# A two-layer encoder trunk on one core: where the differences of weight blocks in the down projection are made and kept

## What is computed

```python
h2 = rms_norm(x, g_ffn_pre[i])
u = causal_dwconv(h2 @ w_up[i], conv_w[i], conv_b[i])
ug, uv = u[..., :D_FF], u[..., D_FF:]
f = (jax.nn.gelu(ug, approximate=True) * uv) @ w_down[i]     # 512 x 2816 times 2816 x 1024
x = x + rms_norm(f, g_ffn_post[i])
```

## Time and profile before

| | |
|---|---|
| median of three runs | 1831.44 us |
| profiled execution, whole | 1827.23 us |
| its span, first to last instruction | 1825.4 us |
| TensorE matmul busy | 1809.3 us (99%) |
| VectorE busy | 1190.9 us (65%) |
| ScalarE busy | 935.3 us (51%) |
| GpSimd busy | 346.0 us (19%) |
| DMA moved | 253.43 MB, mean 139 GB/s |
| mean granted TensorE clock | 0.996 of 2.4 GHz |

### The profile page before, as it was taken

How to read it: one execution, slowest core, us unless ns; L and a number is a source line. 1 busy time by engine, 2 the same in 40 slices (tenths; PEclk the granted TensorE clock), 3 DMA queues, 4 the chain that set the end, 5 groups by cost and what they waited for, 6 DMA issues and landing times.

```text
span 1825.4 us, 26834 instructions
## 1 busy us (share of the span) xinstructions
PE 1809.3 (99%) x9111; PEld 1506.8 (83%) x9111; DVE 1190.9 (65%) x1800; ACT 935.3 (51%) x1660; POOL 346.0 (19%) x314
## 2 busy tenths in 40 slices
PE   9999999999999999999999999999999999999998
PEld 8888888788888888887898888887888888888877
DVE  4756555555577777886656565555455887778874
ACT  4676546533454444555547764466334444445563
POOL 1002001132023334301010020012221244332010
PEclk9999999999999999999999999999999999999999
DMA  6322354479424333685253224545893333337842
GB/s 185 77 82 82 100 115 121 117 192 281 133 80 119 109 118 112 215 286 187 91 150 88 65 82 113 106 130 123 208 275 92 101 109 117 113 116 252 276 143 92
DMA packets 312392, 253.43 MB, mean 139 GB/s; under 512 B 65092, under 2 KB 265440, under 8 KB 312032
## 3 DMA queue, kind: packets, MB, share of 16 engines
q1 hardware_dynamic: 301160, 222.51, 40.6%
q0 software_dynamic: 10752, 29.36, 7.2%
q10 hardware_dynamic: 376, 0.21, 0.1%
HBM read 236.76 MB, written 42.47 MB: 153 GB/s over the span
## 4 chain that ended last, share of the span: by engine, by line
PE 95%; DMA 2%; DVE 2%; issue 0%; ACT 0%; DVEq 0%; POOL 0%; POOLq 0%; ACTq 0%; SPq 0%
PE psum L888 85%; PE psum L1203 2%; DMA raw<-in_w_down_dram 2%; PE psum L1184 2%; PE psum L1169 2%; PE psum L931 1%; PE psum L1156 1%; PE psum L1155 1%; DVE dn_wl L1981 0%; PE psum L1181 0%; PE psum L1166 0%; PE psum L1395 0%; DVE raw L2066 0%; PE psum L1165 0%; DVE dn_ll L1981 0%
## 5 line engine op out<-in xcount | busy, mean ns | idle before, releaser
L888 PE MATMUL psum<-xnh,wh 128*128 128x512 f32 (+1 forms) x1424 | 564.1, 396 | 0.0
L888 PE MATMUL psum<-xnh,wl 128*128 128x512 f32 (+1 forms) x1424 | 548.9, 385 | 0.0
L888 PE MATMUL psum<-xnl,wh 128*128 128x512 f32 (+1 forms) x1424 | 548.3, 385 | 0.0
L1514 ACT ACTIVATE wh<-raw 128x1024 fp32r<-128x1024 f32 (+2 forms) x276 | 284.6, 1033 | 495.3 <-PE psum L888 454.6
L1981 DVE TENSOR_TENSOR wl<-raw,wh 128x1024 fp32r<-128x1024 f32 (+2 forms) x276 | 364.5, 1322 | 150.1 <-ACT wh L1514 149.9
L888 PEld LDWEIGHTS psum<-xnh,wl 128*128 128x128 f32 x1424 | 267.6, 188 | 54.3
L888 PEld LDWEIGHTS psum<-xnh,wh 128*128 128x128 f32 x1424 | 269.1, 189 | 50.1 <-issue 2.7
L888 PEld LDWEIGHTS psum<-xnl,wh 128*128 128x128 f32 x1424 | 268.3, 188 | 46.9
L2219 DVE CUSTOM_DVE_ANT_0 Sp<-psum,ptok 128x128 f32<-128x128 f32 (+3 forms) x128 | 62.8, 491 | 108.4 <-issue 60.3
L2734 POOL TENSOR_TENSOR merged<-merged,th 128x512 f32<-128x512 f32 x32 | 46.8, 1463 | 265.8 <-DVE th L2351 265.7
L2431 DVE TENSOR_TENSOR ub<-psum,rb 128x512 f32<-128x512 f32 x88 | 60.6, 688 | 39.9 <-PE psum L888 39.9
(11 more groups left out here) (333 smaller groups left out, 3477.8 us busy)
## 6 DMA issues: line engine op xcount, KB each, us to landing
raw<-in_w_up_dram SPq DMA_DIRECT2D x88, 512.0 KB, 3.8
raw<-in_w_gate_dram SPq DMA_DIRECT2D x48, 512.0 KB, 3.8
col_sums<-in_w_down_dram POOLq DMA_DIRECT2D x44, 512.0 KB, 8.4
raw<-in_w_down_dram SPq DMA_DIRECT2D x44, 512.0 KB, 4.8
raw<-in_w_in_dram SPq DMA_DIRECT2D x30, 512.0 KB, 3.7
raw<-col_sums SPq DMA_DIRECT2D x22, 512.0 KB, 4.4
qspill<-f_sums SPq DMA_DIRECT2D x22, 384.0 KB, 4.8
q_raw<-qspill SPq DMA_DIRECT2D x22, 384.0 KB, 5.4
```

The costliest lines, as they stand in the source:

```text
L888: ins = pe.matmul(out, left, right, start=start and n == 0, stop=stop and n == 2)
L1514: act.activation(halves(c)[0][:, 0:n], raw[s][:, 0:n], ACT.Copy).then_inc(w_hi.sem, 1)
```

## The change

The difference of the diagonal blocks is made in the first round for pairs 2 to 10 (`DIFF_FROM = 2`), when `dn_raw` is on chip anyway: `lo` calls the new `diff_away`, ahead of its wait for `hi`. The result (128 x 512) goes to one of two buffers `diff_out` at 28 and 30 KB of `in_xn`, which lie over the last part of `ydn`. SyncE stores it to a DRAM tensor `diffs` behind the load four chunks later. In the second round the `dn_diff` chunk of these pairs is loaded from `diffs`, 256 KB instead of 512, and ScalarE takes it as it lands. For pairs 0 and 1 all stays as it was. `threes_taken` waits until all stores have landed, since it writes `ydn`.

```diff
@@
+DIFF_FROM = 2
@@
-    diff_made = Tally(sem("diff_made"), PAIRS)
+    diff_made = Tally(sem("diff_made"), DIFF_FROM)
+    diff_apart = Tally(sem("diff_apart"), PAIRS - DIFF_FROM)
+    diff_kept = [Tally(sem(f"diff_kept{i}"), 16 * len(range(DIFF_FROM + i, PAIRS, 2))) for i in range(2)]
@@
+    diff_out = [in_xn(f"diff_out{i}", 28 + 2 * i, [P, 512]) for i in range(2)]
@@
+    diffs = nc.dram_tensor("diffs", [DEPTH, P, PAIRS, D // 2], F32, kind="Internal").ap()
@@ def chunk_dmas(L, c):
+        if kind == "dn_diff" and m >= DIFF_FROM:
+            return [(r[:, 0:512], diffs[L, :, m, :])]
         if kind in ("dn_raw", "dn_diff"):
@@ def load(L, c):
             wait(w_lo.sem, w_lo.at(L, c - RAW + 1))
+            if CHUNKS[c][0] == "dn_diff" and CHUNKS[c][1] >= DIFF_FROM:
+                k = CHUNKS[c][1] - DIFF_FROM
+                wait(diff_kept[k % 2].sem, diff_kept[k % 2].at(L, 16 * (k // 2 + 1)))
@@ SyncE, behind the loads of q_raw
+                for k in range(PAIRS - DIFF_FROM):
+                    if c == ST_DOWN + 2 * (k + DIFF_FROM) + 4:
+                        wait(diff_apart.sem, diff_apart.at(L, k + 1))
+                        sp.dma_start(diffs[L, :, k + DIFF_FROM, :], diff_out[k % 2][:, :]).then_inc(diff_kept[k % 2].sem, 16)
@@ ScalarE, hi(L, c)
-            if CHUNKS[c][0] == "dn_diff":
+            if CHUNKS[c][0] == "dn_diff" and CHUNKS[c][1] < DIFF_FROM:
                 act.wait_ge(diff_made.sem, diff_made.at(L, CHUNKS[c][1] + 1))
@@ VectorE, lo(L, c)
             if CHUNKS[c][0] == "dn_raw" and CHUNKS[c][1] >= ROWS:
                 rows_sum(L, c)
+            if CHUNKS[c][0] == "dn_raw" and CHUNKS[c][1] >= DIFF_FROM:
+                diff_away(L, c)
             dve.wait_ge(w_hi.sem, w_hi.at(L, c + 1) + it * 4)
@@
+        def diff_away(L, c):
+
+            k, s = CHUNKS[c][1] - DIFF_FROM, (L * NCH + c) % RAW
+            dve.wait_ge(w_landed[s], LAND[L * NCH + c])
+            if k == 0:
+                dve.wait_ge(w_used.sem, w_used.at(L, ST_DOWN))
+            if k >= 2:
+                dve.wait_ge(diff_kept[k % 2].sem, diff_kept[k % 2].at(L, 16 * (k // 2)))
+            dve.tensor_tensor(diff_out[k % 2][:, :], raw[s][:, 0:512], raw[s][:, 512:1024], ALU.subtract
+                              ).then_inc(diff_apart.sem, 1)
@@ def threes_taken(L, a):
             if a == 0:
                 dve.wait_ge(q_lo.sem, q_lo.at(L, PAIRS))
+                for k in range(2):
+                    dve.wait_ge(diff_kept[k].sem, diff_kept[k].at(L, diff_kept[k].per))
@@ def down_chunks(L):
-                if q >= 0 and q % 2 == 0:
+                if q >= 0 and q % 2 == 0 and q // 2 < DIFF_FROM:
                     diff(L, q // 2)
```

## The result

The changed kernel is slower. In one session twelve runs of it gave a median of 1832.67 us (1831.31 to 1834.60) and twelve runs of the kernel before 1829.24 us; the ratio is 1.0020, 95% interval 1.0011 to 1.0029, or +3.4 us. The forecast was 1825.1 us, a gain of 6.3 on the median of 1831.44 shown ahead of it. The profiled execution of the changed kernel took 1833.82 us, its span is 1832.0, and the granted clock is 0.999 in the mean (before 0.996).

What follows compares the result with a forecast made beforehand. TensorE was taken as the bound, with gain possible only at its stalls in the two down-projection tails. A 12.3 us gain less 6.0 us of first-round cost gave -6.3 us, from 1831.4 to 1825.1 us, range 1820.0 to 1834.0.

Steps and rivals of the forecast that it cites:

- the larger of the two and not the sum: First round: delay is the larger of VectorE's and DMA's costs, 4.8 us in the first layer, 4.0 in the second.
- covers of 1.8 and 1.0 us: Turn of the rounds: lo(24) is ready 1.8 and 1.0 us before TensorE wants chunk 24, leaving 3.0 us stall per layer.
- VectorE's own 4.8 us: First round: eight added subtractions at 0.60 us; bounds 4.0 to 4.8 us in the first layer, 2.8 to 4.8 in the second.
- The DMA part: First round: nine 256 KB stores take 6.8 us per layer; free share absorbs some, leaving 4.8 and 3.2 us of delay.
- The ceiling: Both layers' tails: stalls of 3.66 and 4.73 us plus slow-clock losses of 2.7 and 2.4, 13.5 us together.
- The tail: End of the second round: 0.6 us of stall left per layer, slow clock gone; gain 12.3 us.
- The first subtraction: First round: the first of nine falls into VectorE's 1.44 us wait for ScalarE before 753.75 and costs nothing.
- At chunk 6: First round: first TensorE stall, 0.8 us if VectorE and GpSimd take turns, none by shared bandwidth; no change to the total.
- A: Rival, first round: DMA engines have no room, stores cost 6.8 us in each layer; 1829.9 us, chance 0.20.
- C: Rival, turn of rounds: last store lands late, threes_taken waits, one 6.6 us stall lowers the clock; 1837.3 us, chance 0.09.
- D: Rival, tail: not relieved since load 42 goes out no earlier, 0.8 us gained per layer; 1835.8 us, chance 0.09.
- B: Rival, first round: VectorE's idle time hides cost, stalls 4.0 us, tail's 0.6 vanish; 1821.9 us, chance 0.14.

Runs made afterwards that it cites:

- e1: Changed kernel with subtractions whole but each store cut to 8 columns, second round loading 256 KB chunks from w_down: 1826.36 us, ratio 0.9980 to before.
- e2: Changed kernel with the nine stores per layer whole but each subtraction cut to 8 columns: 1829.17 us, ratio 1.0000 to before.
- e3: Changed kernel without subtractions, stores and their waits, second round loading 256 KB chunks from w_down: 1820.30 us, ratio 0.9943 to before.
- e10: Changed kernel without subtractions and stores, second round loading half blocks of w_down, ScalarE's embedding output ahead of its last x_sum: 1817.15 us, ratio 0.9934 to before.
- e8: Changed kernel with seven of eleven 384 KB loads of spilled feature sums per layer cut to 8 columns: 1826.82 us, ratio 0.9987 to before.
- e6: Kernel before, with VectorE in the tail making the column chunk's low half ahead of the next chunk's difference: 1828.78 us, ratio 1.0000.
- e4: Changed kernel with DIFF_FROM = 8, so only the last three pairs' differences are made in the first round: 1829.53 us, ratio 0.9995 to before.
- e9: Changed kernel with DIFF_FROM = 5 (six differences per layer) and ScalarE's embedding output ahead of its last x_sum: 1827.02 us, ratio 0.9989 to before.
- e11: Changed kernel with DIFF_FROM = 6 (five differences per layer) and ScalarE's embedding output ahead of its last x_sum: 1825.11 us, ratio 0.9979 to before.
- e12: Changed kernel with DIFF_FROM = 7 (four differences per layer) and ScalarE's embedding output ahead of its last x_sum: 1824.68 us, ratio 0.9977 to before.

## Why the prediction was wrong

**The step that failed.** It is this one: "DMA and VectorE are filled by the same pace and not one after the other, so I take the larger of the two and not the sum: 4.8 us of delay in the first layer, 4.0 in the second". Measured from the down projection's first matmul, `lo(24)` started after 60.9 us in before and after 69.7 us in the changed kernel:

```profile
801.41 1.23 DVE L2075 TENSOR_TENSOR raw<-raw 128x1024 f32<-128x1024 f32 x1 [1.60 <-DMA raw<-in_w_down_dram]
...
811.62 0.69 DVE L2093 TENSOR_TENSOR raw<-raw 128x512 f32<-128x512 f32 x1 [2.04 <-DMA raw<-in_w_down_dram]
...
814.62 1.81 DVE L1997 TENSOR_TENSOR wl<-raw,wh 128x1024 fp32r<-128x1024 f32 x2
```

That is a delay of 8.8 us, and 7.7 in the second layer. The last row is `lo(24)` itself; the two above show VectorE idle for loads that have not landed, 2.04 us of it ahead of `diff(1)`. With the forecast's covers of 1.8 and 1.0 us the stalls should be 7.0 and 6.7 us; the table has 6.9 and 6.6. The same rule fits e1 (delays 4.3 and 4.1 us, so 2.5 and 3.1; table 2.5 and 3.1) and e2 (5.7 and 5.2, so 3.9 and 4.2; table 3.9 and 4.3). The covers were right, the delay was not. In the second layer the forecast didn't even keep to its own rule: 4.0 lies between VectorE's highest value and DMA's 3.2 and is the larger of no two terms.

**Why the costs add.** Taken against e3, whose second round is the same, the delays of `lo(24)` are 3.2 and 2.5 us by VectorE alone, 4.6 and 3.6 by the stores alone, and 7.6 and 6.1 by both: sums to within 0.2 us. So close a match is partly luck, for e3 itself has `lo(24)` 1.2 and 1.5 us later than before, though it makes the same first round, and e10, with that first round again, 0.5 later and 0.4 earlier; single executions scatter by 1 to 1.5 us. Against before the two alone add up to 10.0 and 9.3, and both together are 8.8 and 7.7. By either reckoning both are 2.5 to 3.1 us above the larger of the two, which is more than the scatter.

Why would they add? What follows is my reading of it. The maximum would hold for two resources that each have their own stock of work. Here there are four `raw` buffers and one circle: `lo` frees a buffer, SyncE issues the load, the load lands, VectorE adds, subtracts and splits, and `lo` frees the buffer. A longer landing and longer work on VectorE are passed one after the other by the same buffer. That the share of the DMA engines stays at 0.95 and VectorE's busy time falls to 37.83 of 40 us fits this. The runs show that the costs add, and e8 that taking other bytes away brings the period back to that of the subtractions alone; that the circle of four buffers is the reason is not shown. A run with a fifth buffer would test it directly; none was made.

**Its terms.** VectorE's own 4.8 us in the first layer was right in size (4.3 in e1; second layer 4.1 in a range of 2.8 to 4.8). The DMA part was forecast at 4.8 and 3.2; e2 has 5.7 and 5.2 against before, 4.6 and 3.6 against e3, so at most a part of it was missing. The rate was not what failed (337 GB/s at a share of 0.99). How much of the free share of 2.0 and 3.6 us took up stores these figures can't tell. The rise in landing time shows the cost of the stores from the side of DMA. Issues of the changed kernel in 757 to 800 (count, KB each, us to landing); the 256 KB loads took 4.8 and the 512 KB ones 5.1 in the same stretch of before:

```profile
raw<-in_w_down_dram SPq DMA_DIRECT2D x14, 256.0 KB, 5.5
raw<-in_w_down_dram SPq DMA_DIRECT2D x6, 512.0 KB, 5.7
diffs<-diff_out SPq DMA_DIRECT2D x7, 256.0 KB, 5.9
```

**A term that was missing.** The embedding's stall, 2.8 us in both layers, stood in no step. In before TensorE came to the embedding 18.6 us behind the start of the tail, held up by the stall and the slow clock; without them it comes 13.5 us behind it, and `ple_out` behind its `x_sum` is late. The forecast let the gain end at the tail and didn't ask what is late next behind it. Against the table the parts add up: the stalls of the first round and the turn are 7.5 us more than forecast, the embedding costs 2.8, and the tail's gain is 1.3 less; that is 11.6 in all, between the forecast's -6.3 and the table's 18.5 - 13.3 = +5.2.

**What was right.** The ceiling: 13.5 us forecast, 13.3 in the table. The tail: 0.6 us of stall left per layer was forecast, 1.2 and 1.1 are, and the clock is at 1.00, the 2.4 GHz level, in both. So the gain is 11.0 us in the tail against a forecast of 12.3, and 8.2 with the embedding's 2.8 taken off (e3, which pays nothing in the first round: 7.8 in the table, 9.6 in the medians). The first subtraction fell into VectorE's idle time: it starts at 752.70, and the idle time ahead of the next split falls from 1.44 to 0.83 us. At chunk 6 the forecast set 0.8 us by turns with GpSimd and none by a shared bandwidth. VectorE in time:

```profile
756.49 1.76 DVE L2075 TENSOR_TENSOR raw<-raw 128x1024 f32<-128x1024 f32 x1
758.17 1.78 DVE L2086 TENSOR_TENSOR diff_out<-raw 128x512 f32<-128x512 f32 x1
759.87 3.98 DVE L1997 TENSOR_TENSOR dn_wl<-raw,dn_wh 128x1024 fp32r<-128x1024 f32 x2
```

The subtraction took 1.78 us, where its median over 18 is 0.69, beside GpSimd operations of 1.7 to 2.3 us, and the first stall of the round is at 762.29, 0.99 us over the pace (1.01 in the second layer). In e2 the subtraction of 8 columns took 1.25 us in this place, and 0.16 in most others. Both operations were 1.09 us longer beside GpSimd, so the wait doesn't shrink with the operation; and e2 has no stall at chunk 6. The Trainium skill (SBUF — State Buffer, Who interferes with whom) has a VectorE `tensor_tensor` with both inputs in SBUF and a GpSimd operation that reads SBUF exclude each other, and the trace agrees in place and size.

Of its signs, the DMA share of the second round fell (0.68 in 806 to 846, before 0.81) and that of the first stayed at 0.95. The sums of rows were to come every 5.5 us instead of every 5.0; they came every 6.4 instead of 5.3 (44.9 and 37.3 us for seven periods), so the 5.0 was misread. Stalls of over 5 us per layer, its sign for A, did show.

**The rivals.** A, with 1829.9 us, came nearer in the number but not in the mechanism: it took the stores for 6.8 us per layer, where e2 has 5.7 and 5.2, and VectorE for nothing on top. The forecast's own two terms, added, were enough, with VectorE's highest value in both layers: 4.8 + 4.8 = 9.6 and 4.8 + 3.2 = 8.0 us of delay, less the covers 7.8 and 7.0 us of stalls, against 6.9 and 6.6 in the table. C is out: the last store, issued at 804.90, landed in 4.5 us, at 809.4, and `threes_taken` started at 812.23, right behind `diff(1)`, which had waited for its load. The Trainium skill (DMA: Bandwidth & Descriptors, Anatomy of one DMA) has the completion of a write to HBM take longest, in a section on DMAs that GpSimd issues; the stores here, which SyncE issues, landed in 5.9 us in the median where loads of the same 256 KB took 5.5, so an excess of 0.4 us agrees with it in sign. The forecast read no excess out of the one `qspill` store, 384 KB in 5.9 us; loads of that size landed in 5.4 in the same stretch of before. D is out, since the tail was relieved; e6 shows that VectorE's order alone brings no time, and e4 that relieving the three tail chunks alone doesn't either. B is out.

**What stays open.** e9, with six differences, measured 1.8 us below before and e11, with five, 4.1, though both lost 9.8 us in the table; their intervals (0.9980 to 0.9998 and 0.9969 to 0.9988) overlap, so no difference between them is shown. The reason why the costs add, and e8's stall at 803.89.

## What to carry to other kernels

Where few buffers circle between a load, an engine and the issue of the next load, add the cost of the engine and the cost of the transfer, each over the whole stretch: here the larger of the two alone was 2.5 to 3.1 us per layer too little. Whether it would be enough with buffers to spare no run here tested. When a stall is taken away, walk on to the next thing that was ready only because of it. And a cost that grows with every moved step and a gain that needs only some of them make a number to choose: here, with ScalarE's embedding output moved as well, four or five moved differences gain over 4 us where nine lose 2.4.

## What the runs showed of the hardware

**The length of a stall alone doesn't tell whether the clock falls.** Two stalls of nearly the same length, one in e12 (second layer, tail) and one in e8 (first layer, first round), TensorE in time and the windows behind them:

```profile
1745.60 0.47 PE L902 MATMUL psum<-dn_lh,qh 128*128 128x512 f32 x1 [2.39 <-ACT dn_lh L1528]
```
```profile
1745.00:1746.00 1.00, 0.40 (x2) 0.39 (x3) 1.00 (x2) 0.00 (x0) 0.00 (x0) 1.00 1.07 414
1746.00:1747.00 1.00, 1.00 (x6) 0.82 (x5) 0.10 (x1) 0.69 (x1) 0.00 (x0) 1.00 0.76 238
```
```profile
803.89 0.47 PE L903 MATMUL psum<-wh,fh 128*128 128x512 f32 x1 [2.41 <-POOL fl L2724]
```
```profile
804.00:806.00 2.00, 2.00 (x6) 1.57 (x7) 0.92 (x2) 0.13 (x1) 0.00 (x0) 0.63 1.03 406
806.00:808.00 2.00, 2.00 (x6) 1.59 (x5) 1.51 (x2) 1.91 (x4) 0.00 (x0) 0.51 0.48 172
```

Behind 2.39 us the granted clock stayed at 1.00, up to 1752 in further windows; behind 2.41 us it was near 0.5, the 1.2 GHz level, for some 4 us, and in e4 behind 1.78 us (843.48) it fell too, to 0.56 in 844 to 846. The forecast had inferred from one stall of 0.69 us that short ones are free; all those of the changed kernel, up to 1.38 us, were.
